# Running maxima of all prompt chunks computed once, gate units in five places of a chunk, the state update after the second value product

## The reference, cut to what matters

```
def mlstm_chunk(carry, blk):
    C0, n0, m0 = carry
    q, k, v, li, lf = blk
    ...
    b = jnp.cumsum(lf, axis=-1)
    ...
    dmat = jnp.where(causal, b[..., :, None] - b[..., None, :] + li[..., None, :], -jnp.inf)
    inter = b + m0[..., None]
    m = jnp.maximum(inter, jnp.max(dmat, axis=-1))
    dexp = jnp.exp(dmat - m[..., None])
    iscale = jnp.exp(inter - m)
    ...
    s = jnp.einsum('bhtd,bhsd->bhts', qs, k) * dexp
    num = iscale[..., None] * jnp.einsum('bhtd,bhdv->bhtv', qs, C0) + jnp.einsum('bhts,bhsv->bhtv', s, v)
    den = iscale * jnp.einsum('bhtd,bhd->bht', qs, n0) + jnp.sum(s, axis=-1)
    h = num / jnp.maximum(jnp.abs(den), jnp.exp(-m))[..., None]
    m_new = m[..., -1]
    w = jnp.exp(b[..., -1:] - b + li - m_new[..., None])
    decay = jnp.exp(b[..., -1] + m0 - m_new)
    C_new = decay[..., None, None] * C0 + jnp.einsum('bhs,bhsd,bhsv->bhdv', w, k, v)
```

## Time and profile before

| | |
|---|---|
| median of 3 runs | 2996.79 us (2996.43 to 2997.97) |
| the profiled execution's own time | 2997.7 us |
| its span in the trace | 2995.9 us |
| mean granted clock of TensorE | 0.986 |
| TensorE busy | 2918.8 us, 97% |
| VectorE busy | 1786.6 us, 60% |
| ScalarE busy | 1392.4 us, 46% |
| GpSimd busy | 648.0 us, 22% |

### The profile page before, as it was taken

One profiled execution on the slowest core, in us unless ns is written; L12 is line 12 of the kernel. 1 busy time (PEld: TensorE's weight loads), 2 busy tenths in 40 slices (PEclk: granted clock), 3 DMA queues, 4 the chain that ended last, 5 costly groups with the idle time before them and its releaser, 6 DMA issues.

```text
span 2995.9 us, 43868 instructions
## 1 busy us (share of the span) xinstructions
PE 2918.8 (97%) x16347; PEld 2777.6 (93%) x16347; DVE 1786.6 (60%) x2655; ACT 1392.4 (46%) x2445; POOL 648.0 (22%) x939
## 2 busy tenths in 40 slices
PE   8999999999999998999999999999999999999997
PEld 7888789888888887999999999999999999999997
DVE  4222247766767655655477764777547775477654
ACT  3222225554555444554355553555535545355443
POOL 1111011111111111221123221232212322134222
PEclk9999989999999998999999999999999999999998
DMA  5342355545554444443434545345443454334433
GB/s 164 124 142 94 98 176 165 173 139 187 187 173 150 137 138 142 138 153 116 153 114 139 155 141 160 113 138 157 143 153 112 143 160 140 121 113 123 132 119 79
DMA packets 245925, 419.71 MB, mean 140 GB/s; under 512 B 38610, under 2 KB 161874, under 8 KB 245714
## 3 DMA queue, kind: packets, MB, share of 16 engines
q1 hardware_dynamic: 243602, 416.77, 44.5%
q10 hardware_dynamic: 2112, 0.13, 0.0%
HBM read 352.12 MB, written 65.74 MB: 139 GB/s over the span
## 4 chain that ended last, share of the span: by engine, by line
PE 61%; DVE 1%; DMA 1%; issue 1%; ACT 1%; SPq 0%; POOL 0%; DVEq 0%; ACTq 0%; POOLq 0%
PE f_ps L1754 41%; PE f_ps L1759 20%; DMA f_sgi<-gate_rows 0%; PE f_st L1766 0%; DVE f_rinv L1972 0%; DMA both_high<-gate_rows 0%; DMA both_high<-in_w_out 0%; ACT f_wh L1816 0%; DVE f_ml L1967 0%; DVE both_low L1976 0%; ACT f_mh L1846 0%; ACT L1825 0%; DVE f_wl L1951 0%; SPq L1689 0%; POOL f_sgi L2113 0%
## 5 line engine op out<-in xcount | busy, mean ns | idle before, releaser
L1951 DVE TENSOR_TENSOR f_wl<-both_high,f_wh 128x1024 fp32r<-128x1024 f32 (+2 forms) x460 | 542.9, 1180 | 140.8 <-ACT f_wh L1816 135.3
L1754 PE MATMUL f_ps<-f_xh,f_wh 128*128 128x416 f32 x1760 | 618.9, 352 | 3.2 <-DVE f_xl L1985 3.2
L1754 PE MATMUL f_ps<-f_xl,f_wh 128*128 128x416 f32 x1760 | 619.2, 352 | 0.0
L1816 ACT ACTIVATE f_wh<-both_high 128x1024 fp32r<-128x1024 f32 (+2 forms) x460 | 442.1, 964 | 281.7 <-PE f_ps L1759 276.9
L1759 PE MATMUL f_ps<-f_xh,f_wl 128*128 128x416 f32 x1760 | 367.9, 351 | 0.0
L1754 PEld LDWEIGHTS f_ps<-f_xh,f_wh 128*128 128x128 f32 x1760 | 330.4, 188 | 11.3 <-DVE f_xl L1985 4.1
L1754 PEld LDWEIGHTS f_ps<-f_xl,f_wh 128*128 128x128 f32 x1760 | 331.4, 188 | 4.0 <-issue 0.6
L1759 PEld LDWEIGHTS f_ps<-f_xh,f_wl 128*128 128x128 f32 x1760 | 329.9, 188 | 2.3
L2004 DVE SCALAR_TENSOR_TENSOR both_high<-both_high,f_taps 128x416 f32<-128x416 f32 (+2 forms) x264 | 154.3, 598 | 296.6 <-ACT both_high L1868 296.4
L1754 PE MATMUL f_ps<-f_gh,f_wh 128*128 128x416 f32 x880 | 310.9, 353 | 5.9 <-issue 5.9
L701 PE MATMUL pp<-gxh,gwh 128*128 128x416 f32 x800 | 302.3, 378 | 12.3 <-DVE gxl L673 12.3
(11 more groups left out here) (251 smaller groups left out, 5123.1 us busy)
## 6 DMA issues: line engine op xcount, KB each, us to landing
both_high<-in_w_up SPq DMA_DIRECT2D x220, 512.0 KB, 3.7
both_high<-in_w_dn SPq DMA_DIRECT2D x120, 384.0 KB, 3.1
both_low<-in_w_gate SPq DMA_DIRECT2D x80, 512.0 KB, 4.0
both_high<-in_w_br SPq DMA_DIRECT2D x40, 512.0 KB, 3.9
both_high<-in_w_out SPq DMA_DIRECT2D x40, 512.0 KB, 3.6
gate_rows<-gsgo SPq DMA_DIRECT2D x98, 208.0 KB, 2.9
f_sgi<-gate_rows SPq DMA_DIRECT2D x52, 208.0 KB, 4.0
proj_rows<-both_high SPq DMA_DIRECT2D x12, 900.0 KB, 4.5
```

Of the source, the lines that this page charges most:

```text
L1754: pe.matmul(ps[n][:, 0:TB], wh[s][:, (col + k) * P:(col + k) * P + P], x[:, k0 + k, :], start=(k == 0 and x is xhi), stop=False)
L1816: act.activation(wh[v % WS][:, 0:w], raw[s][:, 0:w], ACT.Copy).then_inc(ev("w_hi"), 1)
L1951: dve.tensor_tensor(wl[n][:, 0:w], raw[s][:, 0:w], wh[n][:, 0:w].bitcast(F32), ALU.subtract).then_inc(ev("w_lo"), 1)
```

## The change

The running maximum and what follows from it depend on the gates alone, so they can be known for all prompt chunks before the first. The new functions `run_*`, placed in the sample chunk, do that: `acall` of all chunks is transposed to 64 rows (chunk, head) of 128 positions, seven shifted maxima give the running maximum, it is transposed back, its last values are spread to all partitions, 16 steps of two operations carry the maximum from chunk to chunk, and one exponential gives all scales. The negated maxima are transposed, written to HBM (`chunk_maxima`) and read back for each chunk with every row sent to all 128 partitions.

In a prompt chunk this removes `mix_pe_a`, `mix_pe_last`, `mix_pe_str` and their partners on the other engines. The mLSTM matrix is computed transposed at once (keys as rows), multiplied by an exponential made from the loaded maxima, a mask (`mix_dve_mask`) and a bias (`mix_act_decay`), both in place and a chunk ahead. The places for gate units become five, with 2, 2, 2, 3 and 2 halves. The state update goes behind the value product of the second heads, the next chunk's transposes go ahead of `mix_pe_hm`, `mix_dve_c` goes behind `mix_dve_h3`, and `rotate` goes ahead of `mix_dve_h`.

```diff
-SLOTS = (1, 2, 1, 1, 1, 2, 1, 2)
+SLOTS = (2, 2, 2, 3, 2)
...
+        def maxima_load(n):
+            if n > N:
+                return
+            q = (n - 1) % 2
+            wait(sp, "sb_ready", n - 2 if n > S + 1 else S)
+            sp.dma_start(decays[q][:].rearrange("p h t -> p (h t)"), mxs[row_of(n)].partition_broadcast(P)
+                         ).then_inc(ev(f"mr_in{q}"), 16)
...
+            if k == 3:
+                sp.wait_ge(ev("nmt_ready"), 1)
+                sp.dma_start(mxs.rearrange("n (h t) -> (n h) t", h=MH), run[0][0:4 * CHUNKS, 0:P]).then_inc(ev("mxs_out"), 16)
+                sp.wait_ge(ev("mxs_out"), 16)
+                maxima_load(S + 1)
...
             rows_load(n + 1)
+            maxima_load(n + 1)
             units(n, 0)
...
+    def run_pe_rows(pe):
+        pe.wait_ge(ev("acall_ready"), 1)
+        pe.transpose(p3[0:W4, P:2 * P], flat(acall[:, 0:CHUNKS, :]), K("ident")).then_inc(ev("run_tr"), 1)
+    def run_pe_back(pe):
+        pe.wait_ge(ev("run_max"), 7)
+        wait(pe, "am_ready", S)
+        pe.transpose(p3[:, 0:W4], run[1][0:W4, P // 2:P // 2 + P], K("ident", W4)[:, 0:W4]).then_inc(ev("cmx_tr"), 1)
+    def run_pe_last(pe):
+        pe.wait_ge(ev("cmx_ready"), 1)
+        pe.matmul(p3[:, W4:2 * W4], K("last"), flat(cmx[:]), start=True, stop=True)
+        pe.matmul(p3[:, 2 * W4:3 * W4], K("last"), flat(ball[:, 0:CHUNKS, :]), start=True, stop=True).then_inc(ev("lastv_done"), 1)
+    def run_pe_out(pe):
+        pe.wait_ge(ev("nmall_ready"), 1)
+        wait(pe, "st_ready", S)
+        pe.transpose(p3[0:W4, 0:P], flat(nmall), K("ident")).then_inc(ev("nmt_tr"), 1)
...
+    def run_dve_rows(dve):
+        dve.wait_ge(ev("run_tr"), 1)
+        dve.memset(run[0][:, 0:P // 2], NEG)
+        dve.memset(run[1][:, 0:P // 2], NEG)
+        dve.tensor_copy(run[0][0:W4, P // 2:P // 2 + P], p3[0:W4, P:2 * P]).then_inc(ev("run_ready"), 1)
+    def run_dve_max(dve):
+        dve.wait_ge(ev("run_ready"), 1)
+        for i in range(7):
+            src, dst, at = run[i % 2][0:W4], run[1 - i % 2][0:W4], P // 2
+            wait(dve, "run_max", i)
+            dve.tensor_tensor(dst[:, at:at + P], src[:, at:at + P], src[:, at - 2 ** i:at + P - 2 ** i], ALU.max
+                              ).then_inc(ev("run_max"), 1)
...
+    def run_dve_states(dve):
+        dve.wait_ge(ev("lastv_ready"), 1)
+        for c in range(CHUNKS):
+            wait(dve, "m0_step", c)
+            dve.tensor_tensor(mlall[:, c, :], m0all[:, c, :], lastv[:, 0, c, :], ALU.max).then_inc(ev("ml_step"), 1)
+            dve.wait_ge(ev("ml_step"), c + 1)
+            dve.tensor_tensor(m0all[:, c + 1, :], mlall[:, c, :], lastv[:, 1, c, :], ALU.add).then_inc(ev("m0_step"), 1)
+    def run_dve_all(dve):
+        dve.wait_ge(ev("m0_step"), CHUNKS)
+        m0s = m0all[:, 0:CHUNKS, :]
+        dve.tensor_tensor(cmx[:], cmx[:], m0s, ALU.max).then_inc(ev("mx_all"), 1)
+        dve.wait_ge(ev("mx_all"), 1)
+        dve.tensor_scalar(nmall, cmx[:], -1.0, None, ALU.mult).then_inc(ev("nmall_ready"), 1)
+        dve.tensor_tensor(exall[:, 0], m0s, cmx[:], ALU.subtract)
+        dve.scalar_tensor_tensor(exall[:, 1], ball[:, 0:CHUNKS, :], -1.0, cmx[:], ALU.mult, ALU.subtract)
+        dve.tensor_tensor(exall[:, 2], acall[:, 0:CHUNKS, :], mlall[:], ALU.subtract)
+        dve.tensor_tensor(exall[:, 3], m0s, mlall[:], ALU.subtract).then_inc(ev("exall_ready"), 1)
+    def run_dve_scale(dve):
+        dve.wait_ge(ev("exoall_ready"), 1)
+        dve.tensor_scalar(exall[:, 0], exall[:, 0], SCALE, None, ALU.mult).then_inc(ev("iscall_ready"), 1)
+        dve.wait_ge(ev("iscall_ready"), 1)
+        dve.wait_ge(ev("decall_ready"), 1)
+    def run_act_all(act):
+        act.wait_ge(ev("exall_ready"), 1)
+        t = exall[:].rearrange("p a n h -> p (a n h)")
+        act.activation(t, t, ACT.Exp).then_inc(ev("exoall_ready"), 1)
+        act.wait_ge(ev("exoall_ready"), 1)
+        act.activation(decall[0:DK], exall[0:DK, 3, :, 0:4:2], ACT.Copy)
+        act.activation(decall[DK:P], exall[DK:P, 3, :, 1:4:2], ACT.Copy).then_inc(ev("decall_ready"), 1)
+    def run_act_out(act):
+        act.wait_ge(ev("nmt_tr"), 1)
+        act.activation(run[0][0:W4, 0:P], p3[0:W4, 0:P], ACT.Copy).then_inc(ev("nmt_ready"), 1)
...
-            mm = pe.matmul(p67[:, h % 2, P * (h // 2):P * (h // 2) + P], qkt[r:r + DK, h // 2, :],
-                           qkt[r:r + DK, 2 + h // 2, :], start=True, stop=True)
+            rows, cols = (h // 2, 2 + h // 2) if n == S else (2 + h // 2, h // 2)
+            mm = pe.matmul(p67[:, h % 2, P * (h // 2):P * (h // 2) + P], qkt[r:r + DK, rows, :],
+                           qkt[r:r + DK, cols, :], start=True, stop=True)
...
     def mix_pe_str(pe, n, q):
         wait(pe, "sb_ready", n)
         wait(pe, "am_ready", n)
+        pe.wait_ge(ev("lastv_ready"), 1)
...
-        wait(pe, "st_ready", n)
+        rows = st if n == S else sbuf
+        wait(pe, "st_ready", min(n, S))
         wait(pe, "inr_ready", n)
         for h in range(MH):
-            mm = pe.matmul(p67[:, h % 2, DA * (h // 2):DA * (h // 2) + DA], st[:, h, :], va[q][:, h, :],
+            mm = pe.matmul(p67[:, h % 2, DA * (h // 2):DA * (h // 2) + DA], rows[:, h, :], va[q][:, h, :],
                            start=True, stop=True)
         mm.then_inc(ev("intra_done"), 1)
...
     def mix_pe_hm(pe, n, q):
         wait(pe, "hm_ready", n)
-        wait(pe, "st_ready", n)
+        wait(pe, "st_ready", S)
+        wait(pe, "nmt_ready", 1)
...
+    def mix_dve_mask(dve, n, q):
+        dve.wait_ge(ev(f"mr_in{q}"), 16 * ((n - S + 1) // 2))
+        dve.tensor_tensor(decays[q][:], decays[q][:], bc(K("mask_t")[:, None, :], [P, MH, P]), ALU.add
+                          ).then_inc(ev("masked"), 1)
...
-            ins = dve.scalar_tensor_tensor(cst8[:, j, :], cst8[:, j, :], decp[:, j:j + 1], p67[:, 0, DA * j:DA * j + DA],
+            ins = dve.scalar_tensor_tensor(cst8[:, j, :], cst8[:, j, :], decall[:, row_of(n), j:j + 1], p67[:, 0, DA * j:DA * j + DA],
...
+    def mix_act_decay(act, n, q):
+        wait(act, "masked", n - S)
+        for h in range(MH):
+            ins = act.activation(decays[q][:, h, :], decays[q][:, h, :], ACT.Exp, bias=acall[:, row_of(n), h:h + 1])
+        ins.then_inc(ev("dx_ready"), 1)
...
-        act.activation(decp[0:DK, :], wxo[0:DK, 4:8:2], ACT.Copy)
-        act.activation(decp[DK:P, :], wxo[DK:P, 5:8:2], ACT.Copy).then_inc(ev("decp_ready"), 1)
...
         mix_pe_tr(pe, S, 0)
+        run_pe_rows(pe)
         mix_pe_s(pe, S, 0)
         mix_pe_a(pe, S, 0)
         samp_pe_kc(pe)
         units_pe(pe, S, 0)
+        run_pe_back(pe)
         mix_pe_last(pe, S, 0, "last_s")
         samp_pe_scores(pe)
         units_pe(pe, S, 1)
+        run_pe_last(pe)
         mix_pe_str(pe, S, 0)
         samp_pe_inter(pe)
         units_pe(pe, S, 2)
...
         samp_pe_dec(pe)
         mix_pe_intra(pe, S, 0)
         units_pe(pe, S, 3)
+        run_pe_out(pe)
         samp_pe_pv(pe)
         samp_pe_cup(pe)
         units_pe(pe, S, 4)
...
             q = (n - 1) % 2
             mix_pe_scores(pe, n, q, 0)
             mix_pe_s(pe, n, q)
-            mix_pe_a(pe, n, q)
             units_pe(pe, n, 0)
             mix_pe_scores(pe, n, q, 1)
             units_pe(pe, n, 1)
-            mix_pe_last(pe, n, q)
+            mix_pe_ptr(pe, n, q, 0)
+            mix_pe_inter(pe, n, q)
             units_pe(pe, n, 2)
-            mix_pe_ptr(pe, n, q, 0)
-            mix_pe_str(pe, n, q)
-            mix_pe_inter(pe, n, q)
-            units_pe(pe, n, 3)
             mix_pe_pv(pe, n, q, 0)
             mix_pe_intra(pe, n, q)
-            units_pe(pe, n, 4)
             mix_pe_ptr(pe, n, q, 1)
+            units_pe(pe, n, 3)
+            mix_pe_pv(pe, n, q, 1)
             mix_pe_cup(pe, n, q)
-            units_pe(pe, n, 5)
-            mix_pe_pv(pe, n, q, 1)
-            units_pe(pe, n, 6)
-            mix_pe_hm(pe, n, q)
             if n < N:
                 mix_pe_tr(pe, n + 1, 1 - q)
-            units_pe(pe, n, 7)
-
+            mix_pe_hm(pe, n, q)
+            units_pe(pe, n, 4)
...
         mix_dve_max(dve, S, 0, "mask_s")
         samp_dve_q(dve)
         units_dve(dve, S, 0)
+        run_dve_max(dve)
         mix_dve_s(dve, S, 0)
         mix_dve_isc(dve, S, 0)
+        run_dve_back(dve)
         samp_dve_sm(dve)
         mix_dve_last(dve, S, 0)
         units_dve(dve, S, 1)
+        run_dve_last(dve)
         mix_dve_inter(dve, S, 0)
         samp_dve_pn(dve)
+        run_dve_states(dve)
         units_dve(dve, S, 2)
         samp_dve_decs(dve)
         rotate(dve, S + 1, 1)
         mix_dve_h(dve, S, 0)
+        run_dve_all(dve)
         units_dve(dve, S, 3)
         mix_dve_h2(dve, S, 0)
         samp_dve_c(dve)
-        dve.wait_ge(ev("m_out"), 16)
-        dve.memset(m0[:], 0.0).then_inc(ev("m0_clear"), 1)
-        dve.wait_ge(ev("m0_clear"), 1)
+        run_dve_scale(dve)
         mix_dve_h3(dve, S, 0)
         units_dve(dve, S, 4)
```

(47 more changed lines are left out.)

54 lines of the change are left out of this document (38 added, 16 removed).

## The result

The changed kernel takes 3002.59 us (median of 20 runs, 2997.58 to 3006.76), the kernel before 2998.02 beside it (20 runs, 2996.43 to 2999.77). The ratio is 1.0016, 95% interval 1.0009 to 1.0023. The profiled execution of after took 3002.5 us with a span of 3000.7.

A forecast was written before the change was run, and what follows sets the result against it. The mixer phase is bound by what TensorE issues in order. Savings of 29.3 and old stalls of 16.2 against new costs of 13.2, 1.2, 12.3, 21.0 and 5.0 give +7.2 us: 3004.0, range 2982 to 3017.

The forecast's parts named there:

- a draw: Rival, 0.28: in-order stalls come, but gating and span changes stay near 13, or islands save 2.1 a chunk; 2991 to 3002.
- same: Outcome class, chance 0.28: a difference within about 0.2% (6 us), what a measurement can tell from no change.
- slower: Outcome class, chance 0.48: the changed kernel measures slower by more than about 0.2% (6 us).
- What TensorE saves: Prompt chunks: removed broadcast, matmul island and transposes plus merged islands save 1.83 us in each of 16 chunks, -29.3 us.
- Odd chunks: First probabilities: second maximum waits behind rounding and split, so TensorE stalls 1.65 us before the transposes, x 8, +13.2 us.
- Even chunks: First probabilities nearly meet, +1.2 us; last transposes wait for normalised heads behind VectorE's second split in place 3, +12.3 us.
- Changes of span: Chunks 3, 7, 10, 13, 14: late input splits or gating idle TensorE, partly with slow clock; +21.0 us (10 to 26).
- Old stalls: Prompt chunks 2 to 17: all 16.2 us of earlier stalls and slow clock go out of the sum, -16.2 us.
- Sample chunk: Once: seven maxima stall TensorE 2.8 us, plus own transposes, a wait for last values and 32 steps; +5.0 (+2 to +10).
- The clock: TensorE slows after stalls somewhere between 1.41 and 4.56 us; as rival, six more slow stretches, +14, 3018, chance 0.12.
- The rotation: VectorE, moved ahead of the head step: first step takes 0.82 us, not 1.66, no longer meeting GpSimd's squares.
- Cover holds: Rival, 0.24: meeting points mis-timed by a microsecond, 26.7 us of stalls shrink to 10; 2981, up to 2991.

The follow-up runs named there:

- `ten_short`: Against the changed kernel, in chunk 10 alone VectorE's split of the weights in place 3 goes behind the normalised heads; 3001.4 us.
- `cup_early`: Against the changed kernel, the state update's matmuls go back in front of place 3, behind the second transposes; 3015.15 us.

## Why the prediction was right

The forecast was 3004.0, the result 3002.6; its own range began at 3002.8, so it stands at the border to the rival *a draw*. The change of 0.16% is clear of zero (0.09 to 0.23), but under the 0.2% from which the prediction called a kernel slower, so by its own chances it is the "same" of 0.28 and not the "slower" of 0.48. By its steps:

**What TensorE saves, -29.3.** Right in sum: with both stalls ordered away a chunk takes 35.73 to 35.79, against 37.62: 1.83 to 1.89 for the 1.83 put. Its parts missed by 0.1 each way. In the old places an even chunk takes 36.10, so the matmuls that went are worth 1.52 and not 0.87 + 0.23 + 0.53 = 1.63, and merging the islands, with the moves between them, 0.35 and not 0.2.

**Odd chunks, +13.2.** The mechanism was right to the instruction: the split came behind the rounding and the second maximum started at 824.53, 9.15 us after the last gate matmul before the chunk, the 9.15 of the walk. The wait was 1.26, the stall 37.2 - 35.78 = 1.42 with what it takes to refill, 8 x 1.42 = 11.4. I had 1.65.

**Even chunks, +1.2 and +12.3.** No stall at the first probabilities, and 37.1 - 35.75 = 1.35 at the heads, 10.8 in sum, where the two terms held 13.5. The chain took 6.38 (1042.59 less 1036.21, the copy's start less 0.41), where I took 6.49 over from the earlier trace rows, and TensorE had 5.24 us of work in it, not 5.11. The experiments on the two splits show both causes.

**Changes of span, +21.0.** Measured as the excess over an ordinary chunk of the same kind: 5.1 (chunk 3), 1.8 (7), 5.3 (10), 4.2 (13), 5.0 (14), in sum 21.4. The waits were right within 0.4 (3.39 for 3.5, 2.90 for 3.3, 3.25 for 3.4); the total is right because two errors cancel. Chunks 3 and 14 were put 1.3 too dear each, chunk 10 2.3 and chunk 13 0.7 too cheap: in both the slow clock, put at half, came in full. In chunk 10 its price is seen between two traces with the same waits, 42.37 against 39.56, 2.8 us.

**Old stalls, -16.2.** They went, as put.

**Sample chunk, +5.0.** This term was mis-sized. Seven maxima took 2.18 us (2.1 to 2.6 expected) and the wait was 2.65, but I let the clock stand. Of the 9.5 us by which chunk 2 starts later, 0.75 is there before the chunk's first new work; the other 8.7 hold the wait, about 3.2 of slow clock over the sample scores and the first gate matmuls behind them (6.89 us, from 407.63 to 414.52, for what took 3.66 before), and a wait of 1.77 before the per-sample state updates, 0.35 before, of which I had seen 1.1; the 32 steps ahead of it took 6.2 us on VectorE, 6.4 as estimated. In two other traces of the same sample chunk (`ten_short`, `cup_early`) the delay was 5.6 and 5.7, with a clock of 0.68 and 0.69 over the scores where after had 0.50; in the first, 1.5 of these 3.1 us were gained over the scores, the other 1.5 lie ahead of the wait. The prediction's upper end of 10 held it.

From chunk 2 to 17 the prediction's terms sum to +2.2 (15 of the 16 chunks), and the trace gives -2.0; before chunk 2 they are 3.7 short. The two nearly cancel.

**The clock.** The rule that I took from the earlier trace rows, a threshold somewhere between 1.41 and 4.56 us, was too simple (see below). What I put at nothing stayed there: no gate matmul waited for weights, none for the mask or the reloaded maxima. **The rotation** ran in 0.82 as taken.

*Cover holds* did not happen, for the reason given against it: both chains start from an event of TensorE's own. (The 26.7 us of stalls that it names are those of all chunks, not of one.) But its price, 2981 to 2991, is what one reordering alone reaches, 2986.5 or 2989.0. What I didn't see is that the same change with another order of VectorE's splits and maxima and of two steps of ScalarE's, and with one chunk's places changed, is 44.6 us faster.

## What to carry to other kernels

Merging islands of work on the engine that bounds takes away the cover that each hand-written order of the other engines relied on; after such a change, walk every chain that starts at an event of the bounding engine and ends in a wait of it, and move what is not needed soon (here the split of weights for two units later) behind the chain's end. A step that fills a gap which other engines need anyway is nearly free there and costs more than its own length elsewhere. And measure the saving part alone, in the old order: here it showed at once that the new order lost more than the islands gave.
